# Low-half preps moved out of three norms, a pair's values in one group, the last row tile in two token halves

## What is computed

```python
def reference(x, p, positions, ...):
    x = first_block(x, p, ...)      # mix norm, attention and S5, FFN, gated extra input, final norm
    return second_block(x, c, ...)  # RG-LRU, MLA, FFN with a convolution, final norm

# first layer
n = rmsnorm(h, g_mix);  z = n @ w_in          # "n1": the norm and its first products
q = partial_rotary(q, positions)              # sines and cosines of the positions, then scores

# second layer
h = rmsnorm_2(x, norm1_g) * (1 + scale1) + shift1;  proj = h @ w_in    # "nn"
o = softmax(q k^T) v, 16 heads, value width 64                         # "values"
x = x + gate1 * (merged @ w_out)
h2 = rmsnorm_2(x, norm2_g) * (1 + scale2) + shift2                     # "n3"
u = causal_dwconv(h2 @ w_up, ffn_conv_w, ffn_conv_b)
x = x + gate2 * ((silu(u_gate) * u_val) @ w_down)                      # row tiles "dn"
return rmsnorm_2(x, final_g)                                           # "fin"
```

## Time and profile before

| | us |
|---|---|
| timed runs, median (lowest, highest) | 1795.24 (1795.19, 1796.18) |
| the profiled execution | 1792.66 |
| its span, first instruction to last | 1790.9 |
| busy: PE, DVE, ACT, POOL | 1775.9, 1041.1, 789.2, 268.5 |

### The profile page before, as it was taken

The page is one execution under the profiler, slowest core; times in us unless marked ns, Lnnn a source line. Parts: engine busy times, 40 slices in busy tenths (PEclk is TensorE's granted clock), DMA queues, the critical chain, the costliest instruction groups (busy, mean ns, idle before and its releaser), DMA issues.

```text
span 1790.9 us, 20963 instructions
## 1 busy us (share of the span) xinstructions
PE 1775.9 (99%) x8086; PEld 1421.8 (79%) x8086; DVE 1041.1 (58%) x1675; ACT 789.2 (44%) x1248; POOL 268.5 (15%) x349
## 2 busy tenths in 40 slices
PE   9999999999999999999999999999999999999998
PEld 7888888878887888888887678777778788888887
DVE  8864554756566544554478796256544765435543
ACT  6554544524344222222264666356653444224443
POOL 4766536300000000000001110322210000000000
PEclk9999999999999999999999999999999999999999
DMA  6222223134344534554341422421143233233321
GB/s 218 96 87 89 71 89 92 53 114 152 94 147 164 188 141 178 209 189 153 118 135 58 132 92 76 144 66 59 36 164 95 83 94 95 94 94 94 95 94 71
DMA packets 65411, 202.06 MB, mean 113 GB/s; under 512 B 7520, under 2 KB 11872, under 8 KB 65312
## 3 DMA queue, kind: packets, MB, share of 16 engines
q1 hardware_dynamic: 65312, 200.72, 33.8%
HBM read 192.30 MB, written 8.40 MB: 112 GB/s over the span
## 4 chain that ended last, share of the span: by engine, by line
PE 94%; DVE 2%; ACT 2%; issue 0%; DMA 0%; SPq 0%; POOL 0%; ACTq 0%; DVEq 0%; POOLq 0%
PE bank L258 28%; PE bank L260 28%; PE bank L259 28%; PE bank L659 2%; PE bank L687 1%; PE bank L672 1%; PE bank L304 1%; PE bank L356 1%; PE bank L341 1%; DVE wlo L1446 1%; PE bank L537 1%; ACT whi L856 1%; PE bank L386 0%; PE bank L377 0%; PE bank L300 0%
## 5 line engine op out<-in xcount | busy, mean ns | idle before, releaser
L258 PE MATMUL bank<-tiler,whi 128*128 128x512 f32 x2260 | 912.8, 404 | 4.2 <-DVE wlo L1446 2.3
L260 PE MATMUL bank<-tiler,wlo 128*128 128x512 f32 x2260 | 892.9, 395 | 0.0
L259 PE MATMUL bank<-tiler,whi 128*128 128x512 f32 x2260 | 892.6, 395 | 0.0
L856 ACT ACTIVATE whi<-raw 128x1024 fp32r<-128x1024 f32 x284 | 298.8, 1054 | 511.6 <-PE bank L260 502.9
L258 PEld LDWEIGHTS bank<-tiler,whi 128*128 128x128 f32 x2260 | 427.1, 189 | 117.0 <-issue 16.6
L260 PEld LDWEIGHTS bank<-tiler,wlo 128*128 128x128 f32 x2260 | 426.4, 189 | 99.5
L259 PEld LDWEIGHTS bank<-tiler,whi 128*128 128x128 f32 x2260 | 426.9, 189 | 96.2 <-issue 1.7
L1446 DVE TENSOR_TENSOR wlo<-raw,whi 128x1024 fp32r<-128x1024 f32 x263 | 326.7, 1246 | 264.7 <-ACT whi L856 264.4
L2279 POOL TENSOR_TENSOR stat<-stat,scl 128x4 f32<-128x4 f32 x7 | 7.5, 1080 | 748.9 <-DVE stat L1954 428.2
L2270 POOL TENSOR_TENSOR wlo<-raw,whi 128x1024 fp32r<-128x1024 f32 x21 | 49.9, 2378 | 209.5 <-ACT whi L856 209.5
L2218 DVE SCALAR_TENSOR_TENSOR tile<-bank,sm,tile 128x511 f32<-128x511 f32 x42 | 31.5, 750 | 85.8 <-ACT tile L1410 54.1
(11 more groups left out here) (381 smaller groups left out, 1576.2 us busy)
## 6 DMA issues: line engine op xcount, KB each, us to landing
raw<-wst SPq DMA_DIRECT2D x284, 512.0 KB, 3.6
wide<-wadaT SPq DMA_DIRECT2D x52, 512.0 KB, 3.3
tile<-xT SPq DMA_DIRECT2D x16, 256.0 KB, 6.1
spare<-tile SPq DMA_DIRECT2D x16, 256.0 KB, 2.2
tile<-spare SPq DMA_DIRECT2D x16, 256.0 KB, 5.6
out<-tile SPq DMA_DIRECT2D x8, 256.0 KB, 2.5
tile<-gblk SPq DMA_DIRECT2D x5, 256.0 KB, 4.7
us<-tile SPq DMA_DIRECT2D x4, 256.0 KB, 2.0
```

What stands on the lines that cost most here:

```text
L258: e.matmul(bank, whi[:, o:o + 128], hi, start=start, stop=False)
L259: e.matmul(bank, whi[:, o:o + 128], lo, start=False, stop=False)
L260: e.matmul(bank, wlo[:, o:o + 128], hi, start=False, stop=stop).then_inc(*sig("blk", n))
L856: e.activation(whi[:, c % NHL * W:(c % NHL + 1) * W], raw[:, c % NRAW * W:(c % NRAW + 1) * W], ACT.Copy).then_inc(*sig("hi", c))
```

## The change

Five places:

- n1: the two low-half preps leave DVE's loop and stand behind it as one `prep(5 * CB)`, ahead of the angle work (`sincos`).
- nn (with the norm r12 ahead of it): the loop's prep on DVE moves ahead of DVE's wait for `rb`, ACT's first one ahead of its loop.
- n3: the same on DVE; ACT prepares two chunks ahead of its loop; the low half of chunk 222 goes from DVE to POOL.
- values: the four `mtimes` of an odd head up to 13 are called together, behind the side products.
- tail: the last row tile is made for tokens 0 to 255 and then 256 to 511 (66 matmuls of 256 columns instead of 33 of 512), with the output transposes and the totals of the first half between the matmuls of the second; residual, square, root and reciprocal are done per half, the last row's output factor moves from ACT to DVE, and the output tiles leave in another order.

```diff
         def on_pool(c):
-            return first.get(("uq", 0), 10 ** 6) // CB <= c <= first.get(("pm", 2), 0) // CB
+            return first.get(("uq", 0), 10 ** 6) // CB <= c <= first.get(("pm", 2), 0) // CB or c == first.get(("up", 0), 0) // CB + 4
...
+            def half_total(t, bank):
+                e.wait_ge(*at("acc", "fin", 6))
+                for x in range(2):
+                    e.matmul(bank[:, x:x + 1], F(64)[:, 256 * t + 128 * x:256 * t + 128 * x + 128], ones[:, 0:1], start=x == 0,
+                             stop=False, skip_group_check=True)
+                e.wait_ge(*at("sq", "fin", 7, t))
...
-                    if h % 2:
-                        mtimes(h, 0)
-                        mtimes(h, 1)
                     mturn(h, 3)
                     side(h, 6)
                     side(h, 7)
                     if h % 2:
-                        mtimes(h, 2)
-                        mtimes(h, 3)
+                        for kb in range(4):
+                            mtimes(h, kb)
...
-                for m in range(2, 8):
+                for m in range(2, 8 - hf):
...
+            def last(t, ks):
+                to = (B[7] if t else last_bank)[:, 256 * t:256 * t + 256]
+                for k in ks:
+                    n = n0 + k
+                    if t == 0:
+                        if n % CB == 0:
+                            e.wait_ge(*lo_at(n // CB))
...
+                    hi, lo = (R(x)[:, 256 * t:256 * t + 256] for x in ACTS2[k])
+                    e.matmul(to, whi[:, o:o + 128], hi, start=k == 0, stop=False, skip_group_check=True)
+                    e.matmul(to, whi[:, o:o + 128], lo, start=False, stop=False, skip_group_check=True)
+                    ins = e.matmul(to, wlo[:, o:o + 128], hi, start=False, stop=k == 10, skip_group_check=True)
...
+            last(0, range(11))
+            last(1, [0, 1])
+            out_turn(0, 0, [0, 1, 2, 3])
+            out_turn(0, 1, [0, 1, 2, 3])
+            last(1, [2, 3])
+            out_turn(1, 0, [4, 5, 6])
+            out_turn(1, 1, [4, 5, 6])
+            last(1, [4])
+            half_total(0, B[6])
+            last(1, [5, 6])
...
+            last(1, [9, 10])
+            out_turn(1, 2, [4, 5, 6])
+            e.wait_ge(*at("fin", 0))
+            half_total(1, B[4])
...
         def scalar(e):
...
             sums(7)
+            prep(first.get(("in2", 0), 0) + 8)
...
-                if k in (1, 7):
-                    prep(first.get(("in2", 0), 0) + 8 * (k // 4 + 1))
+                if k == 7:
+                    prep(first.get(("in2", 0), 0) + 16)
...
-            prep(first.get(("up", 0), 0))
+            prep(first.get(("up", 0), 0) + 16)
...
-                if k in (1, 7):
-                    prep(first.get(("up", 0), 0) + 8 * (k // 4 + 1))
+                if k == 7:
+                    prep(first.get(("up", 0), 0) + 24)
...
             def modulated(name, rb, w, ops, so, sh, ahead):
                 for k in range(9):
-                    if k == 3:
-                        prep(ahead)
...
-                prep(ahead + 8)
+                prep(ahead)
...
-            scaled("n1", 8, X_RAW, lambda k: col("g_mix", k), B[3], (62, 63, 65), N1, (3, 6))
+            scaled("n1", 8, X_RAW, lambda k: col("g_mix", k), B[3], (62, 63, 65), N1)
+            prep(5 * CB)
             sincos("ang1", F(43), F(44))
...
             diagonal("n3", ST_N3, 25)
+            prep(first.get(("up", 0), 0) + 8)
             e.wait_ge(*at("rb", "n3"))
-            modulated("n3", B[7], CU, N1, S_N2, 24, first.get(("up", 0), 0) + 8)
+            modulated("n3", B[7], CU, N1, S_N2, 24, first.get(("up", 0), 0) + 16)
...
+            for t in range(2):
+                cols = slice(256 * t, 256 * t + 256)
+                e.wait_ge(*at("dn7", t))
+                e.scalar_tensor_tensor(out=F(HS[7])[:, cols], in0=(B[7] if t else B[(p - 1) % 4])[:, cols], scalar=mod[:, 47:48],
+                                       in1=F(HS[7])[:, cols], op0=MUL, op1=ADD).then_inc(*sig("hd7", t))
...
-            for k in (0, 1, 4, 2, 5, 3, 6, 7):
+            for k in (0, 4, 1, 5, 2, 6, 3, 7):
```

More of the change, by code:

```diff
@@ L57 @@
         "angles": "lo_a ang ang1 ang2 rel wts lru_a mod pow bpad masks",
-        "residual": "h_out h_fd h_pg h_o2 h_dn x2 inv fin",
+        "residual": "h_out h_fd h_pg h_o2 h_dn x2 inv fin hd7 gs7",
         "gated": "ap ga_ev mg fu_ev pr_ev mg2_ev mg2 ua",
@@ L217, in program, with out_bank @@
         first, done = {}, {}
+        def out_bank(half_, j):
+            return B[(7 if half_ else 3) if j == 3 else j if half_ else 4 + j]
         def made(name, m):
@@ L279, in total @@
                 ins.then_inc(*sig("tot", name))
[L281 to L292, removed]
+            def half_total(t, bank):
[4 more added lines that the diff above has]
+                e.wait_ge(*at("sq", "fin", 7, t))
+                for x in range(2):
+                    ins = e.matmul(bank[:, x:x + 1], F(66)[:, 256 * t + 128 * x:256 * t + 128 * x + 128], ones[:, 0:1],
+                                   start=False, stop=True, skip_group_check=True)
+                ins.then_inc(*sig("tot", "fin", t))
             def busy(bank, n):
@@ new lines, in out_turn @@
+            def out_turn(half_, j, ms):
+                if half_ and ms[0] == 4:
+                    if j < 3:
+                        e.wait_ge(*at("h_dn", 1, 4 + j))
+                    else:
+                        e.wait_ge(*at("hd7", 1))
+                elif j == 3:
+                    e.wait_ge(*at("hd7", 0))
+                for m in ms:
+                    if m < 7:
+                        e.wait_ge(*at("gs", m))
+                    else:
+                        e.wait_ge(*at("gs7", j // 2))
+                    ins = e.transpose(out_bank(half_, j)[:, m % 4 * 128:m % 4 * 128 + 128],
+                                      F(OG[m])[:, j * 128:(j + 1) * 128], ident[:, :])
+                if ms[-1] % 4 == 3:
+                    ins.then_inc(*sig("otr", half_, j))
@@ new lines, in tensor @@
+            last(0, range(11))
[8 more added lines that the diff above has]
+            last(1, [5, 6])
+            out_turn(1, 0, [7])
+            out_turn(1, 1, [7])
+            out_turn(0, 3, [0, 1, 2, 3])
+            last(1, [7, 8])
+            e.wait_ge(*at("root", "fin", 0))
@@ L1424, in scalar @@
                             e.activation(stat[:, 234:235], scl[:, HALF + 1:HALF + 2], ACT.Sqrt)
[L1425 to L1429, removed]
-            e.activation(st, B[0][:, 508:512], ACT.Sqrt, scale=1.0 / 1024, bias=scl[:, HALF + 1:HALF + 2]).then_inc(*sig("root", "fin"))
-            e.wait_ge(*at("inv", "fin"))
-            for j in range(4):
-                e.wait_ge(*at("otr", 1, j))
-                e.activation(F(OT[4 + j]), B[j], ACT.Copy, scale=stat[:, ST_F + j:ST_F + j + 1]).then_inc(*sig("fin_a", j))
+                        if m < 7:
+                            e.wait_ge(*at("h_dn", 1, m))
+                            square("fin", m, F(HS[m]), 64, (65, 66))
+                            e.activation(F(OG[m]), F(HS[m]), ACT.Copy, scale=col("gf2", m)).then_inc(*sig("gs", m))
+            e.wait_ge(*at("acc", "fin", 5))
+            for t in range(2):
+                cols = slice(256 * t, 256 * t + 256)
+                e.wait_ge(*at("hd7", t))
+                e.activation(F(66)[:, cols], F(HS[7])[:, cols], ACT.Square).then_inc(*sig("sq", "fin", 7, t))
+                e.wait_ge(*at("tot", "fin", t))
+                e.activation(stat[:, ST_F + 2 * t:ST_F + 2 * t + 2], B[4 if t else 6][:, 0:2], ACT.Sqrt, scale=1.0 / 1024,
+                             bias=scl[:, HALF + 1:HALF + 2]).then_inc(*sig("root", "fin", t))
+                e.wait_ge(*at("inv", "fin", t))
+                for j in (2 * t, 2 * t + 1):
+                    e.wait_ge(*at("otr", 1, j))
+                    e.activation(F(OT[4 + j]), out_bank(1, j), ACT.Copy, scale=stat[:, ST_F + j:ST_F + j + 1]).then_inc(
+                        *sig("fin_a", j))
         def vector(e):
@@ L1955, in vector @@
             diagonal("r12", ST_R12, 48)
+            prep(first.get(("in2", 0), 0) + 8)
             e.wait_ge(*at("rb", "r12"))
-            modulated("nn", B[6], SILU, NN, S_GF, 0, first.get(("in2", 0), 0) + 8)
+            modulated("nn", B[6], SILU, NN, S_GF, 0, first.get(("in2", 0), 0) + 16)
             variance("r1", B[5], 1024, ST_R1)
```

52 lines of the change are left out of this document (26 added, 26 removed).

## The result

| | before | changed |
|---|---|---|
| timed runs, median (lowest to highest), 12 each | 1794.57 (1793.03 to 1796.29) | 1797.99 (1796.27 to 1800.21) |
| span of the profiled execution | 1790.9 | 1794.7 |

The account below looks back on a forecast made before the run. TensorE, busy 99%, bounds the kernel. Terms −0.1 − 1.14 − 2.35 − 1.75 + 1.9 sum to −3.44, −1.74 with one clock drop: 1793.5 us from the median 1795.24; 8-in-10 range 1790.0 to 1797.0.

Parts of the forecast that it names:

- n1: Moved low-half preps: angle work 1.4 later, operand waits saved, score wait about 1.4; net −0.1, bounds −1.4 to +0.3.
- nn: One DVE prep leaves the loop, shortening PE's wait at the r1 spread; net −1.14, bounds −1.2 to −0.6.
- n3: Chunk 222's wait goes, new wait of about 1.9 at chunk 224, POOL blocks DVE 0.9; net −1.75.
- Values: Seven odd heads each lose one group of 64-column matmuls, 0.335 each; −2.35, bounds −1.4 and −2.5.
- −2.64: n3's other end: chunk 224 starts 2.64 earlier if POOL and DVE don't block each other.
- The tail: Split last row: 256-column matmuls every 0.125, new wait of 1.95 for chunk 284, four late transfers; net +1.9.
- Rival D: Slower: half-width matmuls in the tail cost a full-width interval; tail +7.0, 1796.9 or, with a drop, 1798.6; chance 0.09.
- The clock: Three new PE waits (score, chunk 224, chunk 284) of 1.4 to 2.0; one taken to draw a drop, 1.7.
- The chance of 0.06 for slower: Over 1798.8 us: upper end of full-interval half-width matmuls, or two clock drops with a dear tail.

Follow-up runs that it names:

- the mended one: Changed kernel with n1 as before and chunks 284 and 224 both prepared earlier: median 1789.99 us, ratio to the kernel before 0.9972.

## Why the prediction was wrong

**n1, the step that failed.** "So the rope step L1643 (54.22, 0.68 long) ends at 56.3 instead of 54.9": the delay of the angle work was right (1.4), the rope's length was taken from before as if it did not depend on when it runs. Three of its products grew by 0.9 to 1.1 each (58.22 + 1.64 = 59.86 for the end, 59.4 without the run's start), since the later rope met POOL's products, which themselves came 2 us earlier than before. The port was priced in n3, from the earlier trace rows, and not asked about where DVE was moved by 1.4 us; POOL's row at 56.30 in the trace of before, not among the rows that the prediction names, had the answer: its first 128x512 product started 1.4 after the rope's end, as much as the rope was to be moved. Nor was 1.4 a safe distance: in five of the eight other profiles with n1 as before it is 0.16 (n1 undone: 54.86 against 54.70), in three 1.4; what sets it stays open. So n1's −0.1, with a bound of +0.3 above, was +4.6 in the two traces (3.0 port, 1.6 clock), 5.9 and 6.3 in two other profiles and 4.7 to 9.2 alone in the timed runs. The Trainium skill's rule from "SBUF — State Buffer", section "SBUF: two separate sides", which the prediction used in n3, covers this too: products with two SBUF inputs against POOL's, blocked for whole instructions. The 1.63 to 1.76 agree, and the run with POOL's products behind the rope shows 0.68.

The rest of n1's account was loose as well: its lower bound of −1.4 leaves out the transposes at 67.7, which wait on DVE and ACT whatever PE wins earlier; in the run with one prep back, whose score waited for nothing, −0.35 was left behind them.

**nn.** −1.14 was forecast, the shift fell by 1.1, and the wait at the r1 spread from the earlier trace rows's 1.93 to 0.8. Right.

**Values.** −2.35 was forecast, −2.1 came: 0.30 for each head instead of 0.335. Right, a little high.

**n3.** −1.75 was forecast with the port, −1.6 came (1.86 to 0.28), with no wait at chunk 222, one of 1.66 at chunk 224 and the first L1545 blocked. That cost 1.0, 0.9 was expected; PE's wait of 0.7 at the third step is that of before (0.6 at the old L1500), kept by the blocked row. Right, and for the reasons given; that the chunk 222 part of it is worth nothing against a prep on DVE was not seen. The "new PE wait of about 1.9" fits the −1.75 that was kept (PE 3.5 earlier at the chunk, less 1.75), not the −2.64 beside which it stands, which leaves 0.9.

**The tail.** +1.9 was forecast, +2.2 came in the trace, 3.0 to 3.2 in the medians, where the clock behind the wait for chunk 284 comes in. The interval of the half-width matmuls is 0.12 (0.125 taken), the wait 1.85 (1.95). Rival D, a full interval for half the width, is out. The terms between the row's end (1785.2) and the first late issue (1788.2) add up to 2.8 at most, not 3.0, a slip of 0.2. The Trainium skill's estimate beside the forecast ("TensorE: Matmul & The Clock Gate", section "Back-to-back issue gap"), 0.109, is further off than 0.125.

**The clock.** One drop of 1.7 was forecast for one of three waits. In the changed kernel's profile there was one, behind the longest wait, which was 4.45 and not the 1.4 forecast for that place; where that wait was 1.44 (POOL behind the rope) full clock followed it. So that the number of drops agrees is luck. Over all profiles the wait for chunk 284 was followed by full clock in some (the changed kernel, n1 undone, chunk 222 on DVE) and by 0.50 in others (POOL behind the rope, chunk 224 early, one prep in n1, the tail alone), at nearly the same length, 1.8 to 1.9: a chance for each wait was the right form. With n1 alone and with the tail undone the stretch at the score was twice as long, 6.8. The waits of before went both ways, too: that at the r1 spread (1.9) was followed by full clock in three of the four profiles that keep it and by 0.50 in the tail alone (966.40 to 969.82), that for chunk 222 (1.8) by 0.50 in three and by full clock in the values alone.

**The range.** With POOL's products behind the rope the same change took 1792.4, inside it and 1.1 from the forecast. The chance of 0.06 for slower, all from the tail and the clock, left out a mechanism whose rows stood in the same trace. PE's slower beat, 1.3 of the 3.8 between the two spans, was in no term either.

## What to carry to other kernels

When a change shifts an engine's work by a microsecond or two, look at what the other engine on the shared port runs in the new place, not only at the queue that moves: a duration read from a trace (0.68 us for a rope product here, 1.63 to 1.76 beside POOL) holds for a moved instruction only where its neighbours in time are the same. Before counting a PE wait as won, look for the next wait on a chain that the edit shortens less; a small wait there already (0.6 us on one line here) says that most of the rest of the gain stops at it. Splitting the last tile bought nothing here until its last weight chunk was prepared earlier, and no more than the whole tile after that.

## What was not expected of the hardware

PE's 512-column matmuls have two beats, that is, times from one start to the next. In the trace of before they start every 0.2324 us on average, but for some 70 us from about 1080 on, where all traces show 0.2333; in the changed kernel they start every 0.2333 from the region of n3 to the tail as well, which is 0.4% and made 1.3 us of the result. Starts in the first beat run through a pattern of seven (0.227 to 0.242), in the second they alternate between 0.229 and 0.238. The second beat was in the last 300 us of seven profiles (the changed kernel, POOL behind the rope, chunk 284 early, chunk 224 early, chunk 222 on DVE, the mended one, the tail alone), the first in the seven others, kernel before included; there it set in within 1400 to 1500 each time. In three of the seven (chunk 284 early, the mended one, the tail alone) it stood from about 560 to 930 as well, which cost another 1.5 to 1.6. The two kinds aren't parted by any edit that was made, and with one profile for each kernel it stays open what sets it; 1.3 to 2.9 us of a comparison of two single profiles here are this, so a profile's span is compared stage by stage.
